# Last output tile of an encoder layer in two halves of 256 tokens, the first half stored feature-major beside the second

## The reference

```python
x = x + 0.5 * swiglu(rmsnorm(x, ffn2_norm[l]), ffn2_w_gate[l], ffn2_w_up[l], ffn2_w_down[l])
return rmsnorm(x, final_norm)

def rmsnorm(x, g):
    y = xf * lax.rsqrt(jnp.mean(xf * xf, axis=-1, keepdims=True) + RMS_EPS)
    return (y * g.astype(F32)).astype(x.dtype)
def swiglu(x, w_gate, w_up, w_down):
    return (jax.nn.silu(x @ w_gate) * (x @ w_up)) @ w_down
```

## Time and profile before

| | |
|---|---|
| median of 3 runs | 1017.68 us (1017.65 to 1017.9) |
| the profiled execution | 1018.17 us, of it the span from first to last instruction 1016.4 us |
| PE busy | 1003.3 us, 99% |
| PEld busy | 804.8 us, 79% |
| DVE, ACT, POOL busy | 532.2, 333.2, 39.6 us |
| granted clock of TensorE | 0.997 over the span |
| chain that ended last | PE 95%, DVE 3%, ACT 1%, issue 1% |

### The profile page before, as it was taken

One profiled execution on the slowest core, in us unless ns is written; L12 is line 12 of the kernel. 1 busy time (PEld: TensorE's weight loads), 2 busy tenths in 40 slices (PEclk: granted clock), 3 DMA queues, 4 the chain that ended last, 5 costly groups with the idle time before them and its releaser, 6 DMA issues.

```text
span 1016.4 us, 11977 instructions
## 1 busy us (share of the span) xinstructions
PE 1003.3 (99%) x4500; PEld 804.8 (79%) x4500; DVE 532.2 (52%) x737; ACT 333.2 (33%) x484; POOL 39.6 (4%) x43
## 2 busy tenths in 40 slices
PE   9999999999999999999999999999999999999996
PEld 8787888888777887676777878788888888888885
DVE  6545444544444438658887755644544544432332
ACT  6323232232222232234544553432232232222222
POOL 0000000000010110000000002200000000001110
PEclk9999999999999999999999999999999999999998
DMA  8432233223333336121221222323233223233312
GB/s 285 147 98 89 87 100 103 88 100 98 94 90 101 94 115 243 52 84 42 81 81 43 108 79 83 104 84 103 86 100 103 84 102 103 80 111 95 94 57 83
DMA packets 34671, 100.89 MB, mean 99 GB/s; under 512 B 3845, under 2 KB 10758, under 8 KB 34380
## 3 DMA queue, kind: packets, MB, share of 16 engines
q1 hardware_dynamic: 33996, 98.38, 30.1%
q0 software_dynamic: 352, 1.85, 0.5%
q10 hardware_dynamic: 288, 0.18, 0.1%
HBM read 96.19 MB, written 4.21 MB: 99 GB/s over the span
## 4 chain that ended last, share of the span: by engine, by line
PE 95%; DVE 3%; ACT 1%; issue 1%; DVEq 0%; POOL 0%; ACTq 0%; POOLq 0%
PE bank L1386 27%; PE bank L1388 27%; PE bank L1387 27%; PE bank L1611 1%; PE bank L1554 1%; PE bank L1708 1%; PE bank L1710 1%; PE bank L1709 1%; PE bank L1585 1%; PE bank L1594 1%; PE bank L1527 1%; DVE w_lo L787 1%; PE bank L1501 1%; DVE x_lo L847 1%; PE bank L1545 0%
## 5 line engine op out<-in xcount | busy, mean ns | idle before, releaser
L1386 PE MATMUL bank<-x_hi,w_hi 128*128 128x512 f32 x864 | 340.7, 394 | 1.9 <-DVE w_lo L787 1.9
L1388 PE MATMUL bank<-x_hi,w_lo 128*128 128x512 f32 x864 | 336.4, 389 | 0.0
L1387 PE MATMUL bank<-x_lo,w_hi 128*128 128x512 f32 x864 | 336.3, 389 | 0.0
L787 DVE TENSOR_TENSOR w_lo<-raw,w_hi 128x1024 fp32r<-128x1024 f32 (+1 forms) x164 | 198.7, 1211 | 201.0 <-ACT w_hi L442 196.7
L442 ACT CAST w_hi<-raw 128x1024 fp32r<-128x1024 f32 (+1 forms) x164 | 168.1, 1025 | 191.4 <-PE bank L1388 180.4
L1386 PEld LDWEIGHTS bank<-x_hi,w_hi 128*128 128x128 f32 x864 | 162.2, 188 | 41.9 <-issue 9.0
L1388 PEld LDWEIGHTS bank<-x_hi,w_lo 128*128 128x128 f32 x864 | 162.2, 188 | 34.1
L1387 PEld LDWEIGHTS bank<-x_lo,w_hi 128*128 128x128 f32 x864 | 162.3, 188 | 33.4 <-issue 0.7
L1386 PE MATMUL bank<-h_hi,w_hi 128*128 128x512 f32 x352 | 137.3, 390 | 0.0
L1388 PE MATMUL bank<-h_hi,w_lo 128*128 128x512 f32 x352 | 137.0, 389 | 0.0
L1387 PE MATMUL bank<-h_lo,w_hi 128*128 128x512 f32 x352 | 136.9, 389 | 0.0
(11 more groups left out here) (229 smaller groups left out, 714.6 us busy)
## 6 DMA issues: line engine op xcount, KB each, us to landing
raw<-in_ffn_w_gate SPq DMA_DIRECT2D x43, 512.0 KB, 3.3
raw<-in_ffn_w_up SPq DMA_DIRECT2D x43, 512.0 KB, 3.4
raw<-in_ffn_w_down SPq DMA_DIRECT2D x32, 512.0 KB, 3.5
raw<-in_w_in SPq DMA_DIRECT2D x24, 512.0 KB, 3.4
raw<-in_ffn_w_down SPq DMA_DIRECT2D x16, 384.0 KB, 3.1
raw<-in_w_out SPq DMA_DIRECT2D x8, 512.0 KB, 4.0
resid<-in_x_t SPq DMA_DIRECT2D x8, 256.0 KB, 5.3
resid_dram<-resid SPq DMA_DIRECT2D x1, 2048.0 KB, 13.8
```

What stands on the lines that cost most here:

```text
L787: nc.vector.tensor_tensor(w_lo[:, half, 0:kb, :], raw[:, slot, 0:kb, :], w_hi[:, half, 0:kb, :].bitcast(F32), ALU.subtract).then_inc(w_spl ...
L1386: nc.tensor.matmul(dst, w_hi[:, half, k, :], hi, start=first and k == 0, stop=False)
L1387: nc.tensor.matmul(dst, w_hi[:, half, k, :], lo, start=False, stop=False)
L1388: ins = nc.tensor.matmul(dst, w_lo[:, half, k, :], hi, start=False, stop=last and k == kb - 1)
```

## The change

The last of the eight output tiles is computed for tokens 0 to 255 first and then for tokens 256 to 511 with the same weights. The third weight chunk of that tile gets buffers of its own (`end_hi`, `end_lo`), since the first two must stay until the second half has used them. The squares of the last tile are not added by GpSimd: TensorE multiplies both `ssq` (seven tiles) and `sq[:, 1]` (the last) with the ones and accumulates. The first half is normalised without being turned: its inverse roots are spread over the partitions by two transposes into bank 0, VectorE makes eight products with `x_fin`, and SP stores them feature-major, in four DMAs with runs of 256 tokens (1 KB). The second half is turned by 16 transposes, ten before its sums and six behind them, scaled by ScalarE and VectorE, and stored in four DMAs, one of them issued by ScalarE. The host puts the two halves of the output together.

```diff
+HALF = S // 2
+END_SUM, END_SPREAD = 4, 9
...
-            o = out[0].rearrange("(t p) d -> p t d", p=P)
-            for t in range(NT):
-                for half, scaled in enumerate((out_even, out_odd)):
-                    sp.wait_ge(scaled, t + 1)
-                    at = slice(4 * half * P, 4 * (half + 1) * P)
-                    sp.dma_start(o[:, t, at], o_nat[:, t, at]).then_inc(stored, 16)
-            sp.wait_ge(stored, 16 * 2 * NT)
+            o = flat[0:D * HALF].rearrange("(j p t) -> p j t", p=P, t=HALF)
+            for j in range(0, KD, 2):
+                sp.wait_ge(out_turned, j + 2)
+                sp.dma_start(o[:, j:j + 2, :], o_turned[:, j:j + 2, :]).then_inc(stored, 16)
+            sp.wait_ge(out_even, 1)
+            sp.dma_start(o_rows[:, 0, 0:4 * P], o_nat[:, 0, 0:4 * P]).then_inc(stored, 16)
+            sp.wait_ge(out_odd, 1)
+            sp.dma_start(o_rows[:, 1, 0:4 * P], o_nat[:, 1, 0:4 * P]).then_inc(stored, 16)
+            sp.wait_ge(out_odd, 2)
+            sp.dma_start(o_rows[:, 1, 4 * P:], o_nat[:, 1, 4 * P:]).then_inc(stored, 16)
+            sp.wait_ge(stored, 16 * (KD // 2 + 4))
...
+            def end_split():            # ScalarE, right behind the cast of the second chunk
+                slot = (N_END - 1) % RAW
+                act.wait_ge(raw_landed[slot], 16 * ((N_END - 1) // RAW + 1))
+                nc.scalar.copy(end_hi[:, 0:CHUNKS[2][1], :], raw[:, slot, 0:CHUNKS[2][1], :]).then_inc(w_hi_made, 1)
...
+            end_square(0)               # ScalarE
+            end_rsqrt(0)
+            end_square(1)
+            end_rsqrt(1)
+            act.wait_ge(end_inv, 2)
+            for half, turned in enumerate((1, 3)):
+                act.wait_ge(fin_turned, turned)
+                nc.scalar.activation(o_nat[:, 0, 4 * half * P:4 * (half + 1) * P], bank[(1, 3)[half]][:], ACT.Copy,
+                                     scale=rcol[:, 6:7]).then_inc(out_even, 1)
+            act.wait_ge(out_even, 2)
+            act.dma_start(o_rows[:, 0, 4 * P:], o_nat[:, 0, 4 * P:]).then_inc(stored, 16)
...
+            end_add(0)                  # VectorE: residual add and x_fin, 256 tokens
+            end_inverse(0)
+            dve.wait_ge(end_spread, 1)
+            dve.wait_ge(fin_set, KD)
+            for j in range(KD):
+                nc.vector.tensor_tensor(o_turned[:, j, :], x_fin[:, j, 0:HALF], bank[0][:, 0:HALF], ALU.mult).then_inc(out_turned, 1)
+            end_add(1)
+            end_inverse(1)
+            dve.wait_ge(end_inv, 2)
+            for half, turned in enumerate((2, 4)):
+                dve.wait_ge(fin_turned, turned)
+                nc.vector.tensor_scalar(o_nat[:, 1, 4 * half * P:4 * (half + 1) * P], bank[(4, 7)[half]][:], rcol[:, 7:8], None,
+                                        ALU.mult).then_inc(out_odd, 1)
...
+            def last_tile():            # TensorE
+                n0 = N_END - 3
+                parts = [(w_hi[:, n0 % SPLIT], w_lo[:, n0 % SPLIT]), (w_hi[:, (n0 + 1) % SPLIT], w_lo[:, (n0 + 1) % SPLIT]),
+                         (end_hi, end_lo)]
+                pe.wait_ge(resid_set, 3 * KD - 2)
+                for half in range(2):
+                    dst, tokens = bank[5 + half][:, 0:HALF], slice(half * HALF, (half + 1) * HALF)
+                    for c, (k0, kb) in enumerate(CHUNKS):
+                        pe.wait_ge(w_split, n0 + c + 1)
+                        hi, lo = parts[c]
+                        for k in range(kb):
+                            f = k0 + k
+                            nc.tensor.matmul(dst, hi[:, k, :], h_hi[:, f, tokens], start=f == 0, stop=False)
+                            nc.tensor.matmul(dst, hi[:, k, :], h_lo[:, f, tokens], start=False, stop=False)
+                            ins = nc.tensor.matmul(dst, lo[:, k, :], h_hi[:, f, tokens], start=False, stop=f == NF - 1)
+                            if half and f == END_SUM:
+                                end_sum(0)
+                            if half and f == END_SPREAD:
+                                spread_end()
...
+            def end_sum(half):
+                pe.wait_ge(ssq_added, 3 * (KD + 1))
+                pe.wait_ge(end_sq, half + 1)
+                dst = bank[(7, 2)[half]]
+                for t in range(2):
+                    at = slice(half * HALF + t * P, half * HALF + (t + 1) * P)
+                    nc.tensor.matmul(dst[:, t:t + 1], ssq[:, at], ones[:, 0:1], start=True, stop=False)
+                    ins = nc.tensor.matmul(dst[:, t:t + 1], sq[:, 1, at], ones[:, 0:1], start=False, stop=True)
+                ins.then_inc(end_summed, 1)
...
-            down(3, 1)
...
+            down(3, 1, last=True)
+            last_tile()
+            turn_end(1, 0, range(4))
+            turn_end(4, 1, range(4))
+            turn_end(3, 0, range(4, 6))
+            end_sum(1)
+            turn_end(7, 1, range(4, 7))
+            turn_end(3, 0, range(6, 8))
+            turn_end(7, 1, range(7, 8))
```

More of the change, by code:

```diff
@@ L196, in build @@
         x_fin, _ = place("x_fin", [P, KD, S], at=x_lo_at)
[L197 removed]
+        o_turned, _ = place("o_turned", [P, KD, HALF], at=x_hi_at)
+        o_nat, _ = place("o_nat", [P, 2, D], at=x_hi_at + 4 * KD * HALF)
+        end_hi, _ = place("end_hi", [P, 8, P], F32R, at=cos_t_at)
+        end_lo, _ = place("end_lo", [P, 8, P], F32R, at=sin_t_at)
         rcol, _ = place("rcol", [P, 8], at=silu_at)
@@ L279, in piece @@
                 raw_landed[n] if part == 2 else early_landed[2 * part + n], 16)
+        flat = out.rearrange("o s d -> (o s d)")
+        o_rows = flat[D * HALF:].rearrange("(t p d) -> p t d", p=P, d=D)
         GAIN = ["ffn1_norm", "mix_norm", "ffn2_norm", "final_norm"]
@@ L407, in squares, with add @@
                 nc.gpsimd.memset(ssq[:], 0.0).then_inc(ssq_added, 1)
[L408 to L412, removed]
+                def add(b, i):
+                    pool.wait_ge(resid_sq, number(KD * (s - 1) + b + 1, 2, i))
+                    pool.wait_ge(ssq_added, number((KD + 1) * (s - 1) + b + 2, 2, i))
+                    nc.gpsimd.tensor_tensor(ssq[:], ssq[:], sq[:, b, :], ALU.add).then_inc(ssq_added, 1)
+                with pool.Fori(0, KD // 2 - (s == 3)) as i:
+                    add(0, i)
+                    add(1, i)
+                if s == 3:
+                    add(0, KD // 2 - 1)
             pool.wait_ge(vec_set, 2)
@@ L501, in down, with end_square, end_rsqrt @@
                     for c in range(3):
-                        if not (last and j == 3 and c == 2):
-                            split(CHUNKS[(c + 1) % 3][1], N_STAGE[s] + 3 * j + c + 1, 12, i)
+                        if last and j == 3 and c > 0:
+                            continue
+                        split(CHUNKS[(c + 1) % 3][1], N_STAGE[s] + 3 * j + c + 1, 12, i)
                         if sines and c == 1 and 4 * i + j in (2, 4, 6):
                             mlp_sin((4 * i + j) // 2 - 1)
+                    if last and j == 3:
+                        end_split()
+                        break
                     resid_block(s, j, 4, i, middle=(lambda: split(8, N_MIX + 1)) if (s, i, j) == (1, 1, 3) else None)
+            def end_split():
+                slot = (N_END - 1) % RAW
+                act.wait_ge(raw_landed[slot], 16 * ((N_END - 1) // RAW + 1))
+                nc.scalar.copy(end_hi[:, 0:CHUNKS[2][1], :], raw[:, slot, 0:CHUNKS[2][1], :]).then_inc(w_hi_made, 1)
+            def end_square(half):
+                part = slice(half * HALF, (half + 1) * HALF)
+                act.wait_ge(end_set, half + 1)
+                act.wait_ge(ssq_added, 2 * (KD + 1) + KD)
+                nc.scalar.activation(sq[:, 1, part], resid[:, KD - 1, part], ACT.Square).then_inc(end_sq, 1)
+            def end_rsqrt(half):
+                act.wait_ge(end_summed, half + 1)
+                nc.scalar.activation(rcol[:, 2 * half:2 * half + 2], bank[(7, 2)[half]][:, 0:2], ACT.Sqrt, bias=eps[:],
+                                     scale=1.0 / D).then_inc(end_root, 1)
             def x_high(j):
@@ L857, in widen_rinv, with end_split, end_add, end_inverse @@
                 dve.wait_ge(rinv_made, s + 1)
+            def end_split():
+                dve.wait_ge(w_hi_made, N_END)
+                nc.vector.tensor_tensor(end_lo[:, 0:CHUNKS[2][1], :], raw[:, (N_END - 1) % RAW, 0:CHUNKS[2][1], :],
+                                        end_hi[:, 0:CHUNKS[2][1], :].bitcast(F32), ALU.subtract).then_inc(w_split, 1)
+            def end_add(half):
+                part = slice(half * HALF, (half + 1) * HALF)
+                if half:
+                    dve.wait_ge(w_used, N_END)
+                else:
+                    dve.wait_ge(end_half, 1)
+                nc.vector.scalar_tensor_tensor(resid[:, KD - 1, part], bank[5 + half][:, 0:HALF], 0.5, resid[:, KD - 1, part],
+                                               ALU.mult, ALU.add).then_inc(end_set, 1)
+                dve.wait_ge(end_set, half + 1)
```

(31 more changed lines are left out.)

25 lines of the change are left out of this document (8 added, 17 removed).

## The result

The changed kernel takes 1016.12 us (median of 18 runs, 1015.78 to 1017.11), the kernel before 1017.83 us in the same comparison (18 runs). The ratio is 0.9981, 95% interval 0.9975 to 0.9988: faster by 0.19%, since the interval does not reach 1. That is 1.7 us gained where 2.1 were forecast, and 0.5 us from the forecast time of 1015.6. The profiled execution took 1015.85 us; its span is 1013.5, granted clock 0.998.

The account below looks back on a forecast made before the run. TensorE's order and what follows its last matmul bound the kernel, with stores bounding the end. The last matmul ends 3.53 us later, the tail takes 7.95 instead of 13.56: 2.1 us shorter, 1015.6 us, range 1014.3 to 1017.2.

Parts of the forecast that it names:

- B: TensorE gives the gain back: 0.126 us a matmul or tail hand-over 0.4 longer, 1016.0 to 1016.4; chance 0.34 with D.
- D: VectorE's second-half add waits behind eight products of 0.6 each, tail 0.5 us later, 1016.1; chance 0.34 with B.
- 1, half the data: Stores at the end: second half's 1.05 MB takes 2.75 us instead of 5.48; first half counted as hidden.
- 2, the tail: From TensorE's last matmul to the end: 7.95 us instead of 13.56, a gain of 5.6 us.
- 3a, the pitch: Last tile on TensorE: 132 matmuls of 256 instead of 66 of 512, 0.120 us each.
- Rival A: Last tile on TensorE: a matmul of 256 takes 0.1134 us; chance 0.22.
- C: Last tile: weight loads set the pitch, at least 0.188 us, median 1023.1 us; chance 0.09.
- 3b, the wait: Last tile's first half: TensorE waits for the second weight chunk from 990.75 to 991.97 us, restarting at 992.11.
- 3c, sum and spread: Inserted among the last tile's matmuls: sum 0.90, two spreads 0.22, slower stretches 0.1, together 1.22 us, without waits.
- From span to median: Whole run: span 2.1 us shorter, taken straight off the median 1017.68, time outside the span unchanged.

Follow-up runs that it names:

- all_sp: Changed kernel with all four stores of the second half issued by SP, none by ScalarE: 1016.19 us.
- halves_only: Kernel before with only the last tile as two halves of 256 tokens, third chunk in its own buffers: 1020.42 us, ratio 1.0032.
- pool_part: Kernel before with only GpSimd's shorter loop (seven squares) and TensorE's longer sum (16 instructions instead of 8): 1019.42 us, ratio 1.0022.
- cast_first: Changed kernel with ScalarE casting the last tile's second chunk before squaring tile 6: 1014.78 us; run again as cast_first_2, 1014.93 us.
- late_spread: Changed kernel with the first half's inverse spread after matmul group 18 instead of 9: 1017.85 us against 1017.87 of the kernel before.
- quarters_only: Kernel before with only the last tile split, as four quarters of 128 tokens (264 matmuls of 128 columns): 1059.63 us.

## Why the prediction was right

The forecast was 1015.6, measured 1016.12, inside the range. The number alone would not have told the forecast from its rivals: B stood at 1016.0 to 1016.4 and D at 1016.1, nearer than the forecast. The trace tells them apart, step by step:

- **1, half the data:** right. 2.76 us against 2.75. VectorE's products ran from N - 4.10 to N - 1.36 (forecast N - 4.2 to N - 1.4), the first half's data had all but ended near N + 1.4.
- **2, the tail:** 7.97 against 7.95. The scaling came at N + 2.78 instead of 2.67, and the data started 0.85 us after the first issue instead of 0.87 and was followed by 0.87 instead of 0.94: small errors that cancel. That the data and not the issue bounds the end is shown by `all_sp`.
- **3a, the pitch:** 0.119 to 0.120 against 0.120 taken. No run on record by then shows the 0.120 for a matmul of 256, nor B's 0.126; both were my estimates. What the runs showed in their place is 0.119 to 0.120, in the changed kernel and in `halves_only`. A matmul of 512 takes (1002.61 - 987.87) / 65 = 0.2268 and half of that is 0.1134, so one of 256 costs 0.006 more than half: the time does not halve with the columns. Rival A (0.1134 a matmul) is out, and so is B's 0.126. So is C, since the weight load at 991.62 starts together with the matmul before its own and the pitch is less than the load's 0.19. The 0.1125 of the earlier trace rows alone could not tell how the time goes with the columns: matmuls of a single column with such a load are 0.112 apart (`pool_part`).
- **3b, the wait:** right in its cause (`cast_first` removes it, and 1.28 us with it) and 0.2 too large: w_lo took 1.49 instead of 1.56, and TensorE went on 0.05 instead of 0.14 after it. The idle time before the chunk is 1.2 us (991.39 - 990.08 - 0.12), as forecast; the profile puts 1.04 of it down to waiting because it lists the matmul before as 0.28 long.
- **3c, sum and spread:** 0.90 and 0.22 (1001.35 against 1000.89 less two pitches), as taken. The 0.1 for a slower stretch behind them did not show: the pitch there is 0.119 to 0.120 too. That slower pitch, (26.68 - 24.37) / 10 = 0.231 instead of 0.2268 for matmuls of 512, was the argument for rival B.
- **Rival D** did not happen and would have: `late_spread`.
- **From span to median:** here the working failed. I took over the time outside the span unchanged. That term was 0 and measured 0.5 us; without it the change would have given 2.2 to 2.4 us. A part of the small distance to the forecast is luck: tile and tail came out 0.3 us better than forecast (2.36 against 2.08), which made up for over half of the missing 0.5. At 0.19% the result is just short of the 0.2% that I had named as what can be told from no change; the interval of 18 runs tells it all the same.
- **The sum of rival B:** its 0.65 gives 1016.25 and its two costs together 1016.65, so its 1016.4 does not follow.

## What to carry to other kernels

When a tile is cut into shorter matmuls, the chunks behind it are wanted sooner: check each producer's order against the new times before counting the cover as free. Here one swap on ScalarE was worth 1.3 us in the trace, three quarters of what the change itself gave. At the end of a kernel, move what does not need the last value ahead of the wait for it, and take the time outside the span as a term of its own.

## What the runs showed of the hardware

fp32r matmuls with a weight load each started 0.2268 us apart at 512 columns (`before`) and 0.119 to 0.120 apart at 256 (`after`), both at a granted clock of 1.00. 256 columns fewer took off 0.107, so some 0.012 would be left at no columns, an estimate by the straight line through these two. That line gives 0.066 at 128 columns, and measured was 0.11 (`quarters_only`, before the clock fell); float32 matmuls of one column with a 128-column load were 0.112 apart (`pool_part`). In the 128-column stream, which had one wait of 1.3 us in it, the granted clock fell to 0.50 and the pitch rose to 0.21, and both stayed there for 48 us though TensorE did not pause in them.

Of a VectorE and a GpSimd operation that overlap, the one that starts second was lengthened in these traces and the one already running was not. Started inside GpSimd's add, w_lo of 1024 columns took 1.49 (`after`) to 1.57 us (`halves_only`) instead of 1.23, and the add kept its 1.3. In `cast_first` w_lo started first and kept 1.23 although the add began 0.57 us after it; there the add took 1.80 instead of 1.30, and end_lo, started inside the add, 1.94 instead of 0.94. Each time the second was longer by its overlap with the end of the first less 0.12 to 0.16 us (in the changed kernel 0.41 of overlap and 0.26 longer, for end_lo 1.12 and 1.00), so in these traces it hardly got on until the first was done. `cast_first_2` shows the same within 0.01 us.

The number of microseconds outside the span was a property of the program here, steady within 0.2 us over dozens of runs: 1.8 in the kernel before (1.74 to 1.84), 2.2 with only GpSimd's list and the sum altered (2.13 to 2.24, `pool_part`), 2.3 with the whole change (2.26 to 2.44).
